# Attention block: the causal mask of odd query tiles added to the forget row by Pool and removed again

## The reference, cut to what matters

```python
F = jnp.cumsum(log_f, axis=1).transpose(0, 2, 1)
def block(args):
    q_i, F_i, b_i = args
    logits = (jnp.einsum('bqhd,bkhd->bhqk', q_i, k).astype(jnp.float32) * scale
              + (F_i[..., :, None] - F[..., None, :]))
    q_pos = b_i * Q_BLOCK + jnp.arange(Q_BLOCK)
    logits = jnp.where(k_pos[None, :] <= q_pos[:, None], logits, -jnp.inf)
    p = jax.nn.softmax(logits, axis=-1).astype(v.dtype)
    return jnp.einsum('bhqk,bkhd->bqhd', p, v)
```

## Time and profile before

| | |
|---|---|
| median of three runs | 2501.45 us (2501.05 to 2506.36) |
| the profiled execution | 2504.1 us, its span 2502.5 us |
| busy share of the span: TensorE, VectorE, ScalarE, Pool | 96%, 77%, 54%, 24% |
| bf16 mask products (line 2063) | 128, of 230 ns each as shown |
| `forgotten` (line 2610) | 128, 92.4 us in sum |

### The profile page before, as it was taken

The page is one execution under the profiler, slowest core; times in us unless marked ns, Lnnn a source line. Parts: engine busy times, 40 slices in busy tenths (PEclk is TensorE's granted clock), DMA queues, the critical chain, the costliest instruction groups (busy, mean ns, idle before and its releaser), DMA issues. The chain is left out here.

```text
span 2502.5 us, 33879 instructions
## 1 busy us (share of the span) xinstructions
PE 2412.6 (96%) x11969; PEld 1983.1 (79%) x11969; DVE 1916.0 (77%) x2471; ACT 1352.5 (54%) x1914; POOL 592.7 (24%) x492
## 2 busy tenths in 40 slices
PE   7999999999999999999899999999999999999999
PEld 4766678678888888786688999898788888878887
DVE  5876668678989989896878888787767666657786
ACT  3243323357777777775676767666424444444332
POOL 2000454143333232332710111110042333400000
PEclk9999999999999999999989999999999999999999
DMA  7778355589878899998521111112432443587864
GB/s 269 224 240 291 108 201 212 227 315 394 338 270 307 307 397 408 397 390 343 197 61 51 51 52 52 51 39 94 152 110 80 152 168 143 184 316 261 302 253 152
DMA packets 181315, 535.36 MB, mean 214 GB/s; under 512 B 17710, under 2 KB 77714, under 8 KB 167880
## 3 DMA queue, kind: packets, MB, share of 16 engines
q1 hardware_dynamic: 163900, 470.20, 51.7%
q0 software_dynamic: 12592, 45.63, 4.8%
q10 hardware_dynamic: 4700, 17.92, 1.8%
HBM read 443.38 MB, written 90.33 MB: 213 GB/s over the span
## 5 line engine op out<-in xcount | busy, mean ns | idle before, releaser
L1756 PE MATMUL psum<-w_high,block_hT_high 128*128 128x512 f32 x576 | 232.5, 404 | 7.1 <-DVE w_low L1374 6.0
L1374 DVE TENSOR_TENSOR w_low<-first_w_up,w_high 128x2048 fp32r<-128x2048 f32 x72 | 186.5, 2628 | 52.2 <-ACT w_high L1368 52.2
L1758 PE MATMUL psum<-w_high,block_hT_low 128*128 128x512 f32 x576 | 225.3, 391 | 0.0
L1757 PE MATMUL psum<-w_low,block_hT_high 128*128 128x512 f32 x576 | 224.8, 390 | 0.0
L1756 PE MATMUL psum<-w_qkv_high,fox_hT_high 128*128 128x384 f32 (+1 forms) x512 | 182.7, 357 | 7.3 <-DVE v_high_low L2650 2.7
L1374 DVE TENSOR_TENSOR w_low<-first_w_gate,w_high 128x2048 fp32r<-128x2048 f32 x74 | 168.8, 2284 | 19.6 <-ACT w_high L1368 19.6
L1470 POOL TENSOR_TENSOR block_out<-block_out,late_rows 128x1024 f32<-128x1024 f32 x35 | 92.7, 2650 | 359.6 <-ACT block_out L1634 359.6
L1368 ACT ACTIVATE w_high<-first_w_gate 128x2048 fp32r<-128x2048 f32 x74 | 141.2, 1912 | 67.9 <-DMA first_w_gate<-in_w_expert_gate 64.1
L1756 PE MATMUL psum<-w_mlp_out_high,hidden_part_high 128*128 128x512 f32 x448 | 174.5, 390 | 2.7 <-DVE hidden L3989 1.8
L1757 PE MATMUL psum<-w_qkv_low,fox_hT_high 128*128 128x384 f32 (+1 forms) x512 | 174.8, 341 | 0.0
L1758 PE MATMUL psum<-w_qkv_high,fox_hT_low 128*128 128x384 f32 (+1 forms) x512 | 174.4, 341 | 0.0
(11 more groups left out here) (521 smaller groups left out, 6750.4 us busy)
## 6 DMA issues: line engine op xcount, KB each, us to landing
first_w_gate<-in_w_expert_gate SPq DMA_DIRECT2D x32, 2048.0 KB, 10.4
first_w_up<-in_w_expert_up SPq DMA_DIRECT2D x32, 2048.0 KB, 10.4
first_w_down<-in_w_expert_down SPq DMA_DIRECT2D x31, 2048.0 KB, 10.5
w_mlp_out_quarters<-in_w_mlp_out SPq DMA_DIRECT2D x78, 512.0 KB, 6.8
hidden_part<-hidden_parts SPq DMA_DIRECT2D x54, 512.0 KB, 4.3
v_aug<-in_w_ada SPq DMA_DIRECT2D x48, 512.0 KB, 5.3
expert_rows<-block_out POOLq DMA_DIRECT2D x34, 512.0 KB, 8.8
v_aug<-in_ada_w SPq DMA_DIRECT2D x32, 512.0 KB, 4.9
```

The source lines that it names most:

```text
L1374: dve.tensor_tensor(wl[:, par, half], raw[kind][:, half], wh[:, par, half].bitcast(F32), ALU.subtract).then_inc(s_wl, 1)
L1756: pe.matmul(out, sh, mh, start=start, stop=False)
L1757: pe.matmul(out, sh, ml, start=False, stop=False)
L1758: return pe.matmul(out, sl, mh, start=False, stop=stop)
```

## The change

The bf16 product of the causal triangle stays for `u = 0` and is left out for `u = 1`. In its place Pool puts the triangle into the row F before `forgotten(n, 1)` reads it, in the 128 columns of the odd tile. Since F has the same content in all partitions and the triangle has not, the 128 columns are then no longer plain, and for the next unit of the same head they are needed plain. So per unit:

- `masked(n)` on Pool copies the 128 columns of F into `plain` (the memory of the forget logits `lz`, free by then) and writes `plain + future` into F. `future` is the causal triangle in fp32, made once in the memory of `w_forget`.
- `unmasked(n)` on Pool copies `plain` back, once `forgotten(n, 1)` is done (`s_add`). It is left out for the last unit of a head (`g = 3`), since F is loaded anew.
- `forgotten(n, 1)` on VectorE waits for `masked(n)` (`s_mk`), and `forgotten(n, 0)` with `g > 0` for `unmasked(n-1)` (`s_un`).

The order in Pool's queue is set out in the diff: in the loop `masked(n)`, `unmasked(n)`, `root`, `masked(n+1)`, `unmasked(n+1)`, `masked(n+2)`, `unmasked(n+2)`, `root`, `masked(n+3)`. In the part before the loop `clear_odd` moves behind `root(4)`.

```diff
--- before.py
+++ after.py
@@ -1831,6 +1831,9 @@
             s_oc, s_o, s_ah, s_wa = sem("a_out_copied"), sem("a_out_added"), sem("a_ahead"), sem("a_w_ahead")
             s_f = [sem("a_F0"), sem("a_F1")]
 
+            future = wf[:].rearrange("p k h -> p (k h)")
+            plain = lz[:].rearrange("p t h -> p (t h)")
+            s_fu, s_pl, s_mk, s_un = sem("a_future"), sem("a_plain"), sem("a_masked"), sem("a_unmasked")
             heads = range(0, NG + QUADS, QUADS)
             z_block, z_batch, y_block = {}, {}, {}
 
@@ -1969,6 +1972,38 @@
                         pool.wait_ge(s_tr, 6)
                         pool.memset(kl[1][:].bitcast(F32), 0.0).then_inc(s_kz, 1)
 
+                    def future_mask():
+                        pool.wait_ge(s_wfl, 1)
+                        pool.memset(future, 0.0).then_inc(s_fu, 1)
+                        pool.wait_ge(s_fu, 1)
+                        pool.affine_select(out=future, in_=future, compare_op=ALU.is_ge, fill=-NEG, base=0,
+                                           pattern=[[-1, P]], channel_multiplier=1).then_inc(s_fu, 1)
+
+                    def masked(n):
+                        if not 0 <= n < NG:
+                            return
+                        i, h, g = where(n)
+                        at = slice((2 * g + 1) * P, (2 * g + 2) * P)
+                        pool.wait_ge(s_f[h], 16 * (i + 2) if i >= 1 else 16 + 16 * (g // 2))
+                        if n == 0:
+                            pool.wait_ge(s_ft, 2)
+                            pool.wait_ge(s_fu, 2)
+                        elif g > 0:
+                            pool.wait_ge(s_un, n - n // QUADS)
+                        else:
+                            pool.wait_ge(s_mk, n)
+                        pool.tensor_copy(plain, F[:, h, at]).then_inc(s_pl, 1)
+                        pool.wait_ge(s_pl, n + 1)
+                        pool.tensor_tensor(F[:, h, at], plain, future, ALU.add).then_inc(s_mk, 1)
+
+                    def unmasked(n):
+                        if not 0 <= n < NG or n % QUADS == QUADS - 1:
+                            return
+                        i, h, g = where(n)
+                        at = slice((2 * g + 1) * P, (2 * g + 2) * P)
+                        pool.wait_ge(s_add, 2 * n + 2)
+                        pool.tensor_copy(F[:, h, at], plain).then_inc(s_un, 1)
+
                     gather(0)
                     gather(1)
                     gather(2)
@@ -1988,17 +2023,46 @@
                     rstd(7)
                     clear_even()
                     root(1)
+                    future_mask()
                     root(2)
                     root(3)
+                    masked(0)
+                    unmasked(0)
+                    masked(1)
+                    unmasked(1)
+                    masked(2)
+                    unmasked(2)
+                    root(4)
+                    masked(3)
                     clear_odd()
-                    root(4)
+                    masked(4)
+                    unmasked(4)
                     root(5)
+                    masked(5)
+                    unmasked(5)
+                    masked(6)
+                    unmasked(6)
                     root(6)
+                    masked(7)
+                    masked(8)
+                    unmasked(8)
+                    masked(9)
+                    unmasked(9)
                     root(7)
+                    masked(10)
+                    unmasked(10)
                     root(8)
+                    masked(11)
                     for n in range(3 * QUADS, NG + QUADS, QUADS):
+                        masked(n)
+                        unmasked(n)
                         root(n // 2 + 3)
+                        masked(n + 1)
+                        unmasked(n + 1)
+                        masked(n + 2)
+                        unmasked(n + 2)
                         root(n // 2 + 4)
+                        masked(n + 3)
 
                 @block.tensor
                 def _(pe):
@@ -2059,8 +2123,10 @@
                         for c in range(0, width, HALF):
                             m = min(HALF, width - c)
                             pe.matmul(bank[b + c // HALF][:, 0:m], qs[i % 2][:, h, at], kh[i % 2][:, h, c:c + m], start=True, stop=False)
-                            pe.matmul(bank[b + c // HALF][:, 0:m], qs[i % 2][:, h, at], kl[i % 2][:, h, c:c + m], start=False, stop=c + m < width)
-                        pe.matmul(bank[b + c // HALF][:, m - P:m], idb[:], cm[:], start=False, stop=True).then_inc(s_lg, 1)
+                            ins = pe.matmul(bank[b + c // HALF][:, 0:m], qs[i % 2][:, h, at], kl[i % 2][:, h, c:c + m], start=False, stop=u == 1 or c + m < width)
+                        if u == 0:
+                            ins = pe.matmul(bank[b + c // HALF][:, m - P:m], idb[:], cm[:], start=False, stop=True)
+                        ins.then_inc(s_lg, 1)
 
                     filled = {(NG - 7, 0): 1, (NG - 6, 2): 1, (NG - 5, 0): 1, (NG - 3, 0): 2, (NG - 2, 2): 1, (NG - 1, 0): 1}
 
@@ -2605,6 +2671,10 @@
                         if j == 2:
                             dve.wait_ge(s_xs[3], 16)
                             dve.wait_ge(s_xs[4], 16)
+                        if u == 1:
+                            dve.wait_ge(s_mk, n + 1)
+                        elif g > 0:
+                            dve.wait_ge(s_un, n - n // QUADS)
                         dve.wait_ge(s_lg, j + 1)
                         b = 2 * (j % 2)
                         dve.tensor_tensor_reduce(probs(n, u), psum[:, b:b + 2, :].rearrange("p b n -> p (b n)")[:, 0:width], F[:, h, 0:width],
```

## The result

The kernel after takes 2512.01 us in the median of 20 runs (2508.03 to 2524.81), the kernel before 2506.91 in 20 beside them (2493.95 to 2511.23). The ratio is 1.003, with a 95% interval of 1.0019 to 1.0041: slower by 0.3%, or by 4.8 to 10.3 us. The forecast was 2512.5, slower; it stood 11 us above the 2501.45 that the first three runs of before gave, and the measured medians are 5.1 us apart. The profiled execution of after has a span of 2515.4 us and a time of 2516.98.

A forecast was written before the change was run, and what follows sets the result against it. TensorE's queue paces the attention stage, with slack on VectorE and Pool. -7.0 + 12.6 + 2.1 + 1.5 + 2.0 = +11.2, say +11 us on a median of 2501.45: 2512.5, range 2496 to 2523.

The forecast's parts named there:

- second site: Mask n+3 behind a root in Pool's queue: forgotten(n+3, 1) 2.04 us late, TensorE stalls 1.05 in each of 12 groups.
- Rival 1: Masks are hidden: VectorE's delay at n+3 stays under 0.99 us, TensorE doesn't notice, kernel faster at 2494; chance 0.13.
- rival 2: About even: stall of 0.4 to 0.6 us at n+3 instead of 1.05, +2 in all, 2503.5; chance 0.25.
- first site: Mask n+1 behind a root: VectorE's norm 1.54 us later, hidden from TensorE by 0.3, paid only at n = 56.
- The saving: Dropped bf16 products on TensorE: 0.135 us each, 52 in blocks 4 to 55, 7.0 us.
- The first blocks: masked(0) behind root(3) costs 2.0 us; masks n = 3 and 5, also behind a root, 2.1 together.
- The tail: Last group with a root, n = 56: TensorE already stalls 1.31 us on the norm, so 1.5 more is paid.
- rivals of contention and clock: Pool and VectorE contend, or a new stall drops TensorE to half its clock; chance 0.15 together.
- rival 3: Pool's copy back and VectorE's norm take turns, adding up to 0.4 us at each of 11 first sites: 2517; chance 0.15.
- stalls of 1.31 us leave the clock alone: Argument against the clock rival: after TensorE stalls of 1.31 us the next product ran at full rate, 0.63 for 0.60.

The follow-up runs named there:

- experiment 2: Kernel after with only masked(n+3) of the loop and masked(11) moved ahead of the root beside it; plain groups 31.39 to 31.50 us, stage 496.17.
- experiment 3: Kernel after with only masked(n+1) of the loop moved ahead of its root; plain groups 32.32 to 32.39 us, stage 502.66.
- experiment 4: Kernel before with the odd tiles' mask products left out, nothing in their place; 2500.14 us, 0.9976 of before.
- experiment 7: Kernel after with two more copies on Pool ahead of each mask's add; plain groups 33.20 to 33.26 us, stage 519.98.
- experiment 1: Kernel after with every mask on Pool ahead of the root beside it, except block 0's; 2502.37 us, 0.9978 of before.
- 8: Kernel after with masks ahead of the roots and block 0 keeping its product on TensorE; 2500.34 us, 0.9982 of before.
- 6: Kernel after with odd tiles' mask products kept on TensorE and Pool adding zeros; 2518.87 us, 1.0063 of before.

## Why the prediction was right

**The sign and the place.** The step that carried the forecast, a mask behind `root` at the second site, is shown: with that one moved the plain group falls by 0.9 us, with the other moved by nothing (experiments 2 and 3). Rival 1 (hidden) falls by the period, rival 2 (a stall of 0.4 to 0.6) by the 0.9 of a plain group and the 0.7 of a fresh one; by the medians alone, 5.1 us apart, its +2 would be nearer than the +11.

**The size of the second site: 1.05 forecast, 0.92 measured in a plain group.** The 0.13 is the size of one misreading. I let copy and add take 0.92 us from the end of `root`; the rows of Pool overlap their ends, and the add ends at 1532.09, 3.47 after the start of `sums` at 1528.62, where I had 1522.69 - 1519.08 = 3.61. The same 0.13 comes back at the first site: 1517.72 - 1514.20 = 3.52, for 3.65. There TensorE also asks 0.1 us later after `sums` than forecast (1519.73 - 1514.20 = 5.53, for 5.43), since the weighing between gives back a product's saving (experiment 4). With both, the slack of 0.3 becomes nearly 0.6, as experiment 7 has it. For fresh groups I took over the plain group's price; they pay some 0.7.

**The saving: 7.0 forecast, about 5 measured.** The term was mis-sized: 0.10 a product in place of 0.135, 0.38 to 0.40 for each group of four, some 5 us for the 13 groups. The mechanism (a short product, and a slow start behind it) stands at each place; what I missed is that the time saved makes TensorE meet VectorE's next result. In the stage as a whole experiment 4 shows 3.1 us less, with one more chance wait for weights than before and with 1.2 us given back in the last group (below).

**The first blocks: mis-sized.** Stalls of 5.15 us were forecast (2.0 for the first mask, 1.05 each for `n` = 3, 5 and 11), 3.3 are found: 1.06 for `masked(0)` (30.44 in experiment 1 less 29.38 in 8), 1.16 for the rest of blocks 0 to 3 (31.60 - 30.44), 0.67 in blocks 4 to 7 and 0.41 in 8 to 11 (after less experiment 1). I had carried the loop's price to places of which I had read no row. And of the 1.16 only some 0.3 is a mask behind a `root`: four traces have this order in these blocks, and they take 31.60 (after), 31.73, 30.77 and 30.63 (experiments 2, 3 and 6). The other 0.8 is the clock. The same stretch, 8.6 to 12.6 us after the stage's first sum, in after and in experiment 3 (busy times and, behind them, the granted clock):

```profile
1283.00:1287.00 4.00, 4.00 (x16) 4.00 (x16) 3.86 (x8) 2.44 (x4) 0.44 (x1) 0.61 0.00 0
```

```profile
1275.92:1279.92 4.00, 4.00 (x26) 3.96 (x25) 3.86 (x8) 2.94 (x7) 0.44 (x1) 0.92 0.00 0
```

**The tail:** 1.5 forecast for `n` = 56; TensorE's idle time went from 1.31 to 2.70, and the group by 1.4 to 1.6.

**What held by luck.** The hit on the median (2512.5 forecast, 2512.01 measured) is one: the forecast stood on three runs of before whose median, 2501.45, was 5.5 us below that of the later 20, and the difference forecast was 11 us where the medians differ by 5.1. The stage bears the forecast out better, and there too errors cancelled. The sum was +11.2 and came out at +10.7, but 1.9 of this is the waits for weights, so the change itself is worth +8.8. The saving was put some 2 us too large; the first blocks were charged 1.9 too much, six plain second sites 0.13 each and five fresh ones some 0.3 each, 2.3 together. The 8.8 lie within the 4.8 to 10.3 us of the medians; with runs that spread over some 17 us I can't say more of why these moved by less than the stage of the one profiled execution.

**The rivals of contention and clock.** Contention is there, and costs nothing: see the last section. The clock took part at both ends: some 0.8 us in blocks 0 to 3 (above), and 0.3 us of the 1.7 at the tail, if TensorE's longer idle time made 1.4.

## What to carry to other kernels

Before moving a step to an idle engine, look at what stands ahead of it in that engine's queue: Pool was nine tenths idle in this stage before, and still a 0.75 us step behind a 1.9 us one turned a gain into a loss, while one line further up the same step was free in the loop. Price a late result where the pacing engine asks for it, not where the waiting engine waits: two sites with equal waits on VectorE cost 0.9 us and nothing. A saving on the pacing engine is worth its full size only until that engine meets the next result of another; lay the two traces row by row to see where it is given back.

## What the runs showed of the hardware

**Pool and VectorE take turns.** In after, two timelines of one stretch, VectorE and Pool:

```profile
1483.41 1.76 DVE L2657 TENSOR_TENSOR w_qkv_low<-w_qkv,w_qkv_high 128x1536 fp32r<-128x1536 f32 x1 [0.45 <-ACT w_qkv_high L2362]
...
1486.51 0.69 DVE L2735 TENSOR_TENSOR qk_rows<-qk_rows,qk_sums 128x512 f32<-128x512 f32 x1
...
1484.46 0.86 POOL L1995 COPY forget_logits<-late_rows 128x128 f32<-128x128 f32 x1
...
1486.65 0.69 POOL L2005 COPY late_rows<-forget_logits 128x128 f32<-128x128 f32 x1 [0.80 <-DVE row_min L2680]
```

Pool's copy takes 0.29 alone. Here it starts beside a VectorE row with two inputs in SBUF and takes 0.86 and 0.69; both times it ends 0.15 us after the VectorE row (1485.17 and 1485.32, 1487.20 and 1487.34). That is rival 3's mechanism, and the trace agrees with the Trainium skill, "SBUF — State Buffer", section Who interferes with whom, that the loser blocks fully. VectorE's norm keeps its 0.69, since it issued first. The other way round shows in a grouped view of the loop, shapes kept apart: `share` of 384 columns has a mean of 414 ns in before and of 523 in after, 12 rows each. Six of after's rows take 0.62 to 0.63 us, each begun 0.11 to 0.12 us after an add on Pool; the others take 0.42.

```profile
L2695 DVE TENSOR_SCALAR late_rows<-late_rows,row_sum 128x384 f32<-128x384 f32 x12 | 6.3, 523 | 0.2
```

```profile
L2625 DVE TENSOR_SCALAR late_rows<-late_rows,row_sum 128x384 f32<-128x384 f32 x12 | 5.0, 414 | 0.2
```

None of it reaches TensorE: the copy back has several us until the next mask, and experiment 1, with all of Pool's work in, is as fast as experiment 4 with none.

**The clock after a stall of 1.4 us.** TensorE's `turn_probs` near the end of the stage, 18.04 us into the group, in before and in experiment 1:

```profile
1741.79 0.52 PE L2086 MATMUL psum<-ident,late_rows 128*128 128x128 f32 x3 [1.38 <-DVE k_low_odd L2682]
```

```profile
1745.02 0.88 PE L2152 MATMUL psum<-ident,late_rows 128*128 128x128 f32 x3 [1.38 <-DVE k_low_odd L2752]
```

The table of stretches has the granted clock (the number behind the engines) from 1741 to 1746 in before and from 1745 to 1747 in experiment 1:

```profile
1741.00:1746.00 5.00, 4.21 (x30) 3.63 (x31) 4.92 (x12) 2.81 (x7) 0.00 (x0) 1.00 1.00 379
```

```profile
1745.00:1747.00 2.00, 1.98 (x7) 1.68 (x7) 1.97 (x6) 0.90 (x2) 0.00 (x0) 0.50 1.01 381
```

The same idle time of 1.38 us leaves the engine at 2.4 GHz in the one and at 1.2 in the other, and there the blocks 56 to 59 take 28.34 us for 26.98. Experiment 4 does the same (0.87, 28.14). In experiments 3 and 8 the drop comes 5.7 us earlier, behind the 1.37 and 1.38 us of unit 57, and the groups take 27.07 and 26.96; in after and experiment 2 it follows the 2.70 us. The two traces of before have no such drop in this group. So my sentence that stalls of 1.31 us leave the clock alone holds for the stall of unit 57 in both traces of before and in experiments 4 and 1 (1.31 and 1.39 us), but not in experiments 3 and 8 (1.37 and 1.38); the length of the stall alone doesn't decide, and what does stays open. Some 1.2 to 1.4 us of the gain of experiments 4 and 1 is lost to it.
